# Scaling in two halves and a later add in a block's two even attentions, and another order with output by halves of tokens in its state space model

## The chip, the cores and the metric

The kernel runs on one core of one Trainium2 chip. The metric is the device time of one execution in microseconds (us). A core has five engines with a queue each: TensorE (PE; matmuls and transposes), VectorE (DVE), ScalarE (ACT), GpSimd (POOL) and SyncE (SP, which issues most DMAs). They run side by side and are held in order by semaphores alone: every instruction may count one up, and an engine waits until one has reached a value. All matmul results land in PSUM, which is four tiles of 1024 columns here (P0 to P3).

## What is computed

Two blocks in sequence, on 1024 tokens of width 1024, in float32. The first is a hybrid mixer (a state space model and a pooling branch), a cross attention and a feed-forward part; the second has an even layer with two kinds of attention of 8 heads each and an odd layer with windowed attention. The change touches the state space model and the attentions of the even layer:

```python
def ssd_chunked(xs, dt, a, bm, cm):          # chunks of 128 tokens, 16 heads of 64
    cb = jnp.einsum("bclgn,bcsgn->bgcls", cc, bc)
    y_diag = jnp.einsum("bghcls,bcsghp->bclghp", cb[:, :, None] * seg, xc)
    states = jnp.einsum("bcsgn,bghcs,bcsghp->bcghpn", bc, decay_states, xc)
...
    y_off = jnp.einsum("bclgn,cbghpn,bghcl->bclghp", cc, prev, jnp.exp(a_cs))
    return (y_diag + y_off).reshape(bsz, s, SSD_HEADS, p)
```

and, with y its result: y + d_skip * xs, times silu(z), an rmsnorm with the gain ssd_norm, and the product with w_out.

```python
def block(qi):                               # the even layer's attentions, per head
    sc = jnp.einsum('bqkgd,bskd->bkgqs', qi, k).astype(jnp.float32) * scale
    p = jax.nn.softmax(sc, axis=-1).astype(v.dtype)
    return jnp.einsum('bkgqs,bskd->bqkgd', p, v)
```

## The kernel before

Each float32 operand of a large product is split in a high part (float32r, copied by ACT: `XH`, `wh`, `PTH`) and a low part (the rest, made by DVE: `XL`, `wl`, `PTL`), and a product is three matmuls: high by high, high by low, low by high. The order of the work of every engine is written out by hand, one method per stage and engine (`pe_ssd`, `dve_ssd` and so on); the engines meet only through named counts, as ("bk", c) on DVE's.

**State space model** (`pe_ssd` L1116, `act_ssd` L1182, `pool_ssd` L1213, `dve_ssd` L1248). A loop over c = -1 to 7, in which n = c + 1 is the chunk prepared and c the chunk computed. PE, in a round: transposes of chunk n of XS into P0 (L280, "tx") and of B into P1; the mask products of n (L1143, "cb"); the product of the incoming state (L1150, "off", into P2); the 32 matmuls inside chunk c (L1104, "in", into P3); the new state of c (L1168, "st", into P2, over "off"); last the transposes of chunk c - 1's result back into P0 (`pe_back` L1108, "back"). P0 serves both transposes, so PE's "tx" of a round waits for the last reader of "back", which is DVE's addition `back(c)` at L1264 ("bk": back transposes plus the skip term, into XS). DVE, in a round: the scaled input of n (L1277), the masks (L1282), the scaled "off" (L1292), two products of the decay with the masks (L1258, "wgh"), y = P3 + off (L1299), the state's addition (L1304, "st"), and `back(c - 1)`. POOL: the decayed state (L1232), the decayed input (L1238), the skip product (L1242), and the gating of XS by silu(z) (L1226, "zx") three chunks behind; the gating of chunk 7 is DVE's (L1267). ACT: the decays, 16 + 2 instructions a chunk (L1206, L1211). SP: in the rounds 0, 1 and 4 it loads the rows of later chunks, in round 3 it reloads H, each behind PE's "in".

**Its output** (`pe_ssd_out` L1316, `act_ssd_out` L1322, `dve_ssd_out` L1349). When all of XS is gated, ACT makes eight high parts XH[:, j, :] of 1024 tokens (L1327), DVE the eight low parts (L1346), then both make the squares for the norm. PE's `pe_linear` (L342) goes through eight slabs of weights; the first two take 48 matmuls of 512 columns each, 6 for each k, and wait for the low part k. Behind the second come the roots of the norm (L453). XL shares its memory with the gates GZ. `pe_pair_by_halves` (L373), used so far by two other stages, does the first two slabs together, first for tokens 0 to 511 and then for 512 to 1023, waiting for the low part (name, k, 0) and (name, k).

**Even attentions** (`pe_attention` L2378, `act_attention` L2498, `dve_attention` L2574, `pool_attention` L2662). 128 blocks of 128 queries (64 for each kind of attention), software-pipelined over rounds n = 0 to 133. PE in round n: `turned(n - 3)`, the transposes of the scaled probabilities (L280: 8 of 128 columns into P2, in two groups d = 0, 1 of four, counted as ("t", n, d)); `scores(n)` (L2409, four matmuls in the first kind, six in the second); a side job in some rounds (`beside`: preparation of the second kind); half of a `values` product for a pair of blocks (L2422, L2423). ACT: the high parts PTH (L2548) of n - 3, the exponential of n - 1 (L2555, which also sums), a side job, and in the even rounds from 6 on the copy of one half of the values' result (L2569). DVE:

```python
for n in range(134):
    at = n - 2     # reciprocal L2641, behind ACT's ("exp", at)
    at = n - 3     # low parts PTL L1517, d = 0, 1
                   # reduction of the scores of n, L2648
                   # side job; weights
    if n % 2 == 0 and 0 <= n - 5 < 128:
        p = (n - 5) // 2
        e.wait_ge(*s.act.to(("half", p)))
        e.tensor_tensor(self.result(p), self.pv(p % 2)[0:64, 0:256], self.half(p % 2), ...)
```

The last statement is the add at L2659 ("o", p); PE's next use of that half of P3 waits for it. POOL scales the 1024 probabilities of a row block in place by the reciprocal, one instruction a block (L2669, ("sc", n)), behind the reciprocal; `turned(n)` waits for it.

Of the kernel before, what the change touches and what calls it, by code (L numbers as in the profile page):

```python
# [126 lines left out]
class Kernel:  # L127
# [988 lines left out]
    def pe_ssd(self, e):  # L1116
        sb, s = self.sb, self.s
        pt, pb, pm, py = self.P
        BC, XS = sb["BC"], sb["XS"]
        e.wait_ge(*s.act.to(("xs", 7)))  # L1120
        self.pe_place(e, 0)
        for c in range(-1, 8):
            n = c + 1
            cs, ns, u = slice(128 * c, 128 * c + 128), slice(128 * n, 128 * n + 128), c % 2
            if n < 8:
                if c > 1:
                    e.wait_ge(*s.dve.to(("bk", c - 2)))
                elif n:
                    e.wait_ge(*s.dve.to(("xc", n - 1)))
                for j in range(8):  # L1130
                    ins = self.turn(e, pt[:, 128 * j:128 * j + 128], XS[:, j, ns])
                ins.then_inc(*s.mm.up(("tx", n)))
                if n:
                    e.wait_ge(*s.act.to(("bt", n - 1)))
                    e.wait_ge(*s.dve.to(("wgh", n - 1, 1)))
                else:
                    self.pe_place(e, 1)
                if n < 7:
                    for g in range(2):
                        ins = self.turn(e, pb[:, 128 * g:128 * g + 128], BC[:, g, ns])  # L1140
                    ins.then_inc(*s.mm.up(("tb", n)))
                for g in range(2):
                    ins = e.matmul(pb[:, 512 + 128 * g:640 + 128 * g], BC[:, g, ns], BC[:, 2 + g, ns], start=True,  # L1143
                                   stop=True)
                ins.then_inc(*s.mm.up(("cb", n)))
            if c > 0:
                e.wait_ge(*s.dve.to(("st", c - 1)))
                for g in range(2):
                    gs = slice(512 * g, 512 * g + 512)
                    ins = e.matmul(pm[:, gs], BC[:, 2 + g, cs], sb["ST"][:, gs], start=True, stop=True)  # L1150
                ins.then_inc(*s.mm.up(("off", c)))
            if c >= 0:
                if c:
                    e.wait_ge(*(s.dve if c > 1 else s.act).to(("y", c - 1)))
                else:
                    self.pe_place(e, 3)
                self.pe_inside(e, c, 0)
                self.pe_inside(e, c, 1)
            if 0 <= c < 7:
                e.wait_ge(*s.act.to(("bt", c)))  # L1160
                e.wait_ge(*s.pool.to(("xd", c)))
                if c:
                    e.wait_ge(*s.dve.to(("yt", c)))
                else:
                    self.pe_place(e, 2)
                for g in range(2):
                    gs = slice(512 * g, 512 * g + 512)
                    ins = e.matmul(pm[:, gs], sb["BT"][u][:, 128 * g:128 * g + 128], sb["XD"][u][:, gs], start=True,  # L1168
                                   stop=True)
                ins.then_inc(*s.mm.up(("st", c)))  # L1170
            if c > 0:
                if n < 8:
                    e.wait_ge(*s.dve.to(("xc", n)))
                else:
                    e.wait_ge(*s.dve.to(("bk", c - 2)))
                self.pe_back(e, c - 1)
        e.wait_ge(*s.dve.to(("bk", 6)))
        self.pe_back(e, 7)
        self.emptied = {0: [(s.dve, ("bk", 7))], 1: [(s.act, ("bt", 6)), (s.dve, ("wgh", 7, 1))], 2: [(s.dve, ("yt", 7))],
                        3: [(s.dve, ("y", 7))]}  # L1180
# [67 lines left out]
    def dve_ssd(self, e):  # L1248
# [9 lines left out]
            e.tensor_tensor(x, x, cb, ALU.mult).then_inc(*s.dve.up(("wgh", n, g)))  # L1258

        def back(c):  # L1260
            x = XS[:, :, 128 * c:128 * c + 128]
            e.wait_ge(*s.mm.to(("back", c)))
            e.wait_ge(*s.pool.to(("skip", c)))
            e.tensor_tensor(x, pt.rearrange("p (j l) -> p j l", j=8), x, ALU.add).then_inc(*s.dve.up(("bk", c)))  # L1264
            if c == 7:
                e.wait_ge(*s.dve.here())
                e.tensor_tensor(x, x, self.sb["GZ"][:, :, 896:1024], ALU.mult).then_inc(*s.dve.up(("zx", 7)))  # L1267

        e.wait_ge(*s.act.to("tokens"))
        for c in range(-1, 8):  # L1270
# [25 lines left out]
            if c > 0:  # L1296
                e.wait_ge(*s.mm.to(("in", c, 1)))
                e.wait_ge(*s.dve.to(("yt", c)))
                e.tensor_tensor(YT, py, YT, ALU.add).then_inc(*s.dve.up(("y", c)))  # L1299
            if 0 <= c < 7:  # L1300
                e.wait_ge(*s.mm.to(("st", c)))
                if c:
                    e.wait_ge(*s.pool.to(("stm", c)))
                    e.tensor_tensor(ST, pm, sb["STM"][:, :], ALU.add).then_inc(*s.dve.up(("st", c)))  # L1304
                else:
                    e.tensor_copy(ST, pm).then_inc(*s.dve.up(("st", c)))
            if c > 0:
                back(c - 1)
        back(7)


# [4 lines left out]
    def pe_ssd_out(self, e):  # L1316
        between = {1: lambda e: self.pe_roots(e, "n1", self.T[2], self.s.dve.to(("n1", "sum", 7))),
                   2: lambda e: self.pe_spread(e, "n1", self.T[2])}
        self.pe_linear(e, "so", self.XH, self.XL, lambda k: [(self.s.lo, ("o", k))],
                       lambda j: [(self.s.dve, ("so", j))], between=between)  # L1320

    def act_ssd_out(self, e):  # L1322
        XS = self.sb["XS"]
        e.wait_ge(*self.s.pool.to(("zx", 6)))
        e.wait_ge(*self.s.dve.to(("zx", 7)))
        for j in range(8):
            e.activation(self.XH[:, j, :], XS[:, j, :], ACT.Copy,  # L1327
                         scale=self.vec("ssd_norm", j)).then_inc(*self.s.hi.up(("o", j)))
        for j in range(8):
            self.act_square(e, "n1", j, XS[:, j, :])  # L1330

        def empty(e, j):
            for i in {0: (), 1: (), 2: (0, 1, 2)}.get(j, (j,)):
                e.wait_ge(*self.s.dve.to(("h1", i)))
                e.dma_start(self.dr["hT"][:, i, :], self.H[:, i, :]).then_inc(*self.s.m[i // 4].up("out" if i % 4 == 3 else None))
                self.act_square(e, "n2", i, self.H[:, i, :])
                e.activation(self.AH[:, i, :], self.H[:, i, :], ACT.Copy,
                             scale=self.vec("xattn_norm", i)).then_inc(*self.s.hi.up(("x2", i)))

        between = {1: lambda e: self.act_roots(e, "n1", self.P[3][:, 0:8], 0, D, self.s.mm.to(("n1", "roots"))),  # L1340
                   2: lambda e: self.act_spread(e, "n1", self.T[3])}
        self.act_tiles(e, "so", empty, between)

    def dve_scaled_low(self, e, name, lo, src, gain, hi):
        e.wait_ge(*self.s.hi.to(name))
        e.scalar_tensor_tensor(out=lo, in0=src, scalar=gain, in1=hi.bitcast(F32), op0=ALU.mult,  # L1346
                               op1=ALU.subtract).then_inc(*self.s.lo.up(name))

    def dve_ssd_out(self, e):  # L1349
        XS = self.sb["XS"]  # L1350
        for j in range(8):
            self.dve_scaled_low(e, ("o", j), self.XL[:, j, :], XS[:, j, :], self.vec("ssd_norm", j), self.XH[:, j, :])
        for j in range(8):
            self.dve_square(e, "n1", j)

# [1022 lines left out]
    def pe_attention(self, e):  # L2378
        s = self.s
# [6 lines left out]
        def turned(n):  # L2386
            for d in range(2):
                if n:
                    e.wait_ge(*s.lo.to(("pt", n - 1, d)))
                elif d == 0:  # L2390
                    self.pe_place(e, 2)
                e.wait_ge(*s.pool.to(("sc", n)))
                for k in range(4):
                    c = 512 * d + 128 * k
                    ins = self.turn(e, self.P[2][:, c:c + 128], self.px(n)[:, c:c + 128])
# [178 lines left out]
    def dve_attention(self, e):  # L2574
# [59 lines left out]
        for n in range(134):  # L2634
            at = n - 2
            if 0 <= at < 128:
                w = sb["WST"][at % 4]
                e.wait_ge(*s.act.to(("exp", at)))
                if at > 3:
                    e.wait_ge(*s.pool.to(("sc", at - 4)))  # L2640
                e.reciprocal(w[:, 2:3], w[:, 1:2]).then_inc(*s.dve.up(("inv", at)))  # L2641
            at = n - 3
            if 0 <= at < 128:
                for d in range(2):
# [8 lines left out]
            for i, position in self.WEIGHTS.items():  # L2653
                if position == n:
                    self.dve_weights(e, self.no[i])
            if n % 2 == 0 and 0 <= n - 5 < 128:
                p = (n - 5) // 2
                e.wait_ge(*s.act.to(("half", p)))
                e.tensor_tensor(self.result(p), self.pv(p % 2)[0:64, 0:256], self.half(p % 2),  # L2659
                                ALU.add).then_inc(*s.dve.up(("o", p)))  # L2660

    def pool_attention(self, e):  # L2662

        s = self.s
        for n in range(128):
            r = self.sb["WST"][n % 4][:, 2:3].to_broadcast([128, 1024])
            e.wait_ge(*s.act.to(("exp", n)))
            e.wait_ge(*s.dve.to(("inv", n)))
            e.tensor_tensor(self.px(n), self.px(n), r, ALU.mult).then_inc(*s.pool.up(("sc", n)))  # L2669

    def dve_gate(self, e, j):
        O = self.sb["O"][:, j, :]
# [878 lines left out]
```

## Time and profile before

| what | us |
|---|---|
| median of 3 runs (lowest to highest) | 3027.79 (3027.22 to 3028.67) |
| profiled execution | 3027.36 |
| its span | 3025.5 |
| PE busy | 2891.0, 96% |
| DVE busy | 1731.7, 57% |
| ACT busy | 1243.9, 41% |
| POOL busy | 423.2, 14% |

Times in the profile are counted from the span's start. The state space loop takes about 467 to 562, the even attentions 1927 to 2408. "Busy" of an engine says how much of the span it ran an instruction; the time of the kernel goes by the chain of waits. A row's "[0.88 <-POOL T L2669]" says that the engine sat idle for 0.88 us just before, until POOL's instruction of line 2669 released it. Granted clock 1.00 is 2.4 GHz for PE, 0.50 is 1.2 GHz.

### The profile page before, as it was taken

How to read it: one execution, taken by the hardware profiler on the slowest of the kernel's cores; microseconds unless marked ns; L12 is line 12 of the kernel's file. 1: busy time of each engine (PE TensorE's matmuls, PEld its weight loads, DVE VectorE, ACT ScalarE, POOL GpSimd, SP SyncE). 2: the span in 40 equal slices, each digit the busy share in tenths (PEclk: the TensorE clock that was granted, in tenths of full speed). 3: DMA queues.
4: the chain of work that ended last, by engine and by line, in shares of the span. 5: the costliest groups of instructions: out<-in, count | busy, mean ns of one | idle time of the engine just before them, and what ended most of it. 6: DMA issues, size and time to landing. Idle time of an engine off the chain costs nothing.

```text
span 3025.5 us, 37063 instructions
## 1 busy us (share of the span) xinstructions
PE 2891.0 (96%) x14578; PEld 2413.6 (80%) x14578; DVE 1731.7 (57%) x2258; ACT 1243.9 (41%) x2028; POOL 423.2 (14%) x352
## 2 busy tenths in 40 slices
PE   8999998899999999999999999998999899999998
PEld 6877886687888888888888777787888787888976
DVE  6564476663554444444444745688888835317874
ACT  5221456332443111111112335577767724427851
POOL 0000005200000000000000000255544300004520
PEclk9999999999999999999999999999999999999999
DMA  4111334032222233322331222100001212131031
GB/s 145 56 42 50 126 105 184 26 118 84 91 63 72 73 91 98 92 81 75 87 93 42 76 88 63 56 1 5 15 15 39 98 59 88 49 91 57 22 112 70
DMA packets 226587, 219.28 MB, mean 72 GB/s; under 512 B 9456, under 2 KB 195056, under 8 KB 224880
## 3 DMA queue, kind: packets, MB, share of 16 engines
q1 hardware_dynamic: 214752, 174.90, 18.5%
q0 software_dynamic: 6912, 25.17, 2.8%
q10 hardware_dynamic: 4752, 16.84, 1.5%
q8 instruction: 118, 1.93, 0.3%
q14 instruction: 53, 0.43, 0.0%
HBM read 180.12 MB, written 34.67 MB: 71 GB/s over the span
## 4 chain that ended last, share of the span: by engine, by line
PE 86%; DVE 7%; ACT 3%; issue 2%; POOL 2%; DMA 0%; SPq 0%; ACTq 0%; DVEq 0%; POOLq 0%
PE P L342 61%; PE P L280 5%; PE P L2409 3%; PE P L311 2%; POOL T L2669 2%; PE P L283 1%; PE P L285 1%; PE P L284 1%; PE P L2423 1%; PE P L1104 1%; PE P L2422 1%; DVE PTL L1517 1%; DVE WST L2648 1%; PE P L3010 1%; PE P L1552 1%
## 5 line engine op out<-in xcount | busy, mean ns | idle before, releaser
L267 DVE TENSOR_TENSOR wl<-wf,wh 128x1024 fp32r<-128x1024 f32 (+4 forms) x239 | 251.6, 1053 | 923.8 <-ACT wh L259 923.5
L259 ACT ACTIVATE wh<-wf 128x1024 fp32r<-128x1024 f32 (+4 forms) x239 | 219.8, 920 | 1030.1 <-PE P L342 985.6
L342 PE MATMUL P<-AQ,wh 128*128 128x512 f32 x1824 | 489.4, 390 | 5.8 <-issue 3.0
L342 PE MATMUL P<-XH,wh 128*128 128x512 f32 (+1 forms) x1264 | 396.1, 395 | 8.9 <-DVE XL L1346 5.2
L342 PEld LDWEIGHTS P<-AQ,wh 128*128 128x128 f32 x1824 | 341.3, 188 | 77.9 <-issue 4.6
L342 PE MATMUL P<-XL,wh 128*128 128x512 f32 (+1 forms) x1264 | 391.2, 391 | 0.0
L342 PE MATMUL P<-XH,wl 128*128 128x512 f32 (+1 forms) x1264 | 391.2, 391 | 0.0
L2669 POOL TENSOR_TENSOR T<-T,WST 128x1024 f32<-128x1024 f32 x128 | 242.6, 1895 | 573.8 <-DVE WST L2641 573.8
L342 PEld LDWEIGHTS P<-XH,wh 128*128 128x128 f32 (+1 forms) x1264 | 235.7, 187 | 65.5 <-issue 14.6
L342 PE MATMUL P<-AQ,wl 128*128 128x512 f32 x912 | 280.8, 389 | 0.0
L342 PEld LDWEIGHTS P<-XL,wh 128*128 128x128 f32 (+1 forms) x1264 | 236.2, 187 | 52.6
L342 PEld LDWEIGHTS P<-XH,wl 128*128 128x128 f32 (+1 forms) x1264 | 236.1, 187 | 52.4
L342 PEld LDWEIGHTS P<-AQ,wl 128*128 128x128 f32 x912 | 171.2, 188 | 35.8
L1517 DVE TENSOR_TENSOR PTL<-P,PTH 128x512 fp32r<-128x512 f32 x256 | 164.7, 684 | 53.8 <-ACT PTH L2548 52.7
L342 PE MATMUL P<-FF,wh 128*128 128x512 f32 x680 | 182.4, 390 | 2.1 <-issue 2.0
L2548 ACT ACTIVATE PTH<-P 128x512 fp32r<-128x512 f32 x256 | 139.4, 595 | 84.4 <-PE P L280 81.8
L280 PE MATMUL P<-consts,T 128*128 128x128 f32 x1112 | 147.9, 277 | 26.4 <-POOL T L2669 23.5
L1698 POOL DMA_DIRECT2D AW<-ada_w x48 | 25.6, 534 | 996.4 <-DVE AA L1710 522.1
L2648 DVE TENSOR_REDUCE WST<-P 128x1 f32<-128x1024 f32 x128 | 155.7, 1217 | 2.2 <-PE P L2409 1.9
L280 PEld LDWEIGHTS P<-consts,T 128*128 128x128 f32 x1112 | 125.6, 142 | 38.5 <-DVE PTL L1517 22.2
L342 PEld LDWEIGHTS P<-FF,wh 128*128 128x128 f32 x680 | 127.3, 188 | 29.5 <-issue 2.9
L2555 ACT ACTIVATE T<-P,WST 128x1024 f32<-128x1024 f32 x128 | 143.4, 1120 | 0.1
(438 smaller groups left out, 5006.2 us busy)
## 6 DMA issues: line engine op xcount, KB each, us to landing
AW<-ada_w POOLq DMA_DIRECT2D x48, 512.0 KB, 4.1
wf<-w_gate_up SPq DMA_DIRECT2D x44, 512.0 KB, 3.8
H<-scratch_h SPq DMA_DIRECT2D x32, 512.0 KB, 6.5
wf<-w_in SPq DMA_DIRECT2D x28, 512.0 KB, 3.8
scratch_h<-H SPq DMA_DIRECT2D x24, 512.0 KB, 5.7
scratch_g<-T ACTq DMA_DIRECT2D x22, 512.0 KB, 3.0
wf<-odd_w_in SPq DMA_DIRECT2D x20, 512.0 KB, 3.8
wf<-even_w_in SPq DMA_DIRECT2D x17, 512.0 KB, 3.8
```

The lines of the kernel that those rows point to most:

```text
L259: e.activation(self.sb["wh"][i % 2][:, 0:m], self.sb["wf"][i % 2][:, 0:m], ACT.Copy).then_inc(*self.s.w_hi.up(i))
L267: e.tensor_tensor(l, f, h.bitcast(F32), ALU.subtract).then_inc(*self.s.w_lo.up(i))
L280: return e.transpose(out, in_, self.sb["consts"][p0:p0 + n, a + p0:a + p0 + n])
L283: e.matmul(out, wh, xh, start=first, stop=False)
L311: ins = e.matmul(self.P[slots[j]][:, t:t + 512], w, x[:, k, t:t + 512], start=first and k == 0, stop=last and k == kb - 1)
L342: ins = e.matmul(self.P[slot][0:m, t:t1], w, x[:, k, t:t1], start=first and k == 0, stop=last and k == kb - 1)
L1517: e.tensor_tensor(lo, src, hi.bitcast(F32), ALU.subtract).then_inc(*self.s.lo.up(name))
L2409: ins = e.matmul(p[:, ks], a[:, qs], c[:, ks], start=m == 0, stop=m == len(passes) - 1)
L2548: e.activation(self.probs("PTH", at, d), self.turned(d), ACT.Copy).then_inc(*s.hi.up(("pt", at, d)))
L2555: e.activation(self.px(at), self.P[at % 2], ACT.Exp, bias=w[:, 0:1], accum_out=w[:, 1:2]).then_inc(*s.act.up(("exp", at)))
L2648: e.tensor_reduce(sb["WST"][n % 4][:, 0:1], self.P[n % 2], AX, ALU.max, negate=True).then_inc(*s.dve.up(("max", n)))
L2669: e.tensor_tensor(self.px(n), self.px(n), r, ALU.mult).then_inc(*s.pool.up(("sc", n)))
```

## The change

In the state space loop PE does the transposes back of chunk c - 1 ahead of the new state of c, and DVE the addition `back(c - 1)` ahead of the state's addition. The output is made by halves of tokens: ACT makes eight high halves for tokens 0 to 511 as soon as PE has done "in" of chunk 7 and POOL has gated chunk 3, and eight more when everything is gated; DVE makes the low halves, the first four in between its last steps of the loop; PE takes the first two slabs of weights by halves. In the even attentions POOL scales in two instructions of 512 elements, each with its own count, PE's group d of transposes waits for half d, and the add of pair p moves on DVE from the end of round 2p + 6 to round 2p + 7, behind the reciprocal and ahead of the low parts. The number of instructions grows by 8 on ACT, 8 on DVE and 128 on POOL.

```diff
@@ pe_ssd
                 self.pe_inside(e, c, 0)
                 self.pe_inside(e, c, 1)
+            if c > 0:
+                if n < 8:
+                    e.wait_ge(*s.dve.to(("xc", n)))
+                else:
+                    e.wait_ge(*s.dve.to(("bk", c - 2)))
+                self.pe_back(e, c - 1)
             if 0 <= c < 7:
...
                 ins.then_inc(*s.mm.up(("st", c)))
-            if c > 0:
-                if n < 8:
-                    e.wait_ge(*s.dve.to(("xc", n)))
-                else:
-                    e.wait_ge(*s.dve.to(("bk", c - 2)))
-                self.pe_back(e, c - 1)
@@ dve_ssd, back(c)
             if c == 7:
-                e.wait_ge(*s.dve.here())
+                self.dve_out_low(e, 0, 2)
+                self.dve_out_low(e, 0, 3)
+                e.wait_ge(*s.dve.to(("bk", 7)))
                 e.tensor_tensor(x, x, self.sb["GZ"][:, :, 896:1024], ALU.mult).then_inc(*s.dve.up(("zx", 7)))
@@ dve_ssd
                 e.tensor_tensor(YT, py, YT, ALU.add).then_inc(*s.dve.up(("y", c)))
+            if c == 7:
+                self.dve_out_low(e, 0, 0)
+            if c > 0:
+                back(c - 1)
             if 0 <= c < 7:
...
-            if c > 0:
-                back(c - 1)
+        self.dve_out_low(e, 0, 1)
         back(7)
@@ pe_ssd_out
-        self.pe_linear(e, "so", self.XH, self.XL, lambda k: [(self.s.lo, ("o", k))],
-                       lambda j: [(self.s.dve, ("so", j))], between=between)
+        emptied = lambda j: [(self.s.dve, ("so", j))]
+        self.pe_pair_by_halves(e, "so", "o", emptied, {}, between)
+        self.pe_linear(e, "so", self.XH, self.XL, None, emptied, between=between, start=2)
@@ act_ssd_out
-        e.wait_ge(*self.s.pool.to(("zx", 6)))
-        e.wait_ge(*self.s.dve.to(("zx", 7)))
-        for j in range(8):
-            e.activation(self.XH[:, j, :], XS[:, j, :], ACT.Copy,
-                         scale=self.vec("ssd_norm", j)).then_inc(*self.s.hi.up(("o", j)))
+        e.wait_ge(*self.s.mm.to(("in", 7, 1)))
+        e.wait_ge(*self.s.pool.to(("zx", 3)))
+        for h in range(2):
+            ts = self.half_of(h)
+            if h:
+                e.wait_ge(*self.s.pool.to(("zx", 6)))
+                e.wait_ge(*self.s.dve.to(("zx", 7)))
+            for j in range(8):
+                e.activation(self.XH[:, j, ts], XS[:, j, ts], ACT.Copy,
+                             scale=self.vec("ssd_norm", j)).then_inc(*self.s.hi.up(("o", j) if h else ("o", j, 0)))
@@ dve_out_low (new) and dve_ssd_out
+    def dve_out_low(self, e, h, j):
+        ts = self.half_of(h)
+        self.dve_scaled_low(e, ("o", j) if h else ("o", j, 0), self.XL[:, j, ts], self.sb["XS"][:, j, ts],
+                            self.vec("ssd_norm", j), self.XH[:, j, ts])
...
+        for j in range(4, 8):
+            self.dve_out_low(e, 0, j)
         for j in range(8):
-            self.dve_scaled_low(e, ("o", j), self.XL[:, j, :], XS[:, j, :], self.vec("ssd_norm", j), self.XH[:, j, :])
+            self.dve_out_low(e, 1, j)
@@ pe_attention, turned(n)
-                e.wait_ge(*s.pool.to(("sc", n)))
+                e.wait_ge(*s.pool.to(("sc", n, d)))
@@ dve_attention
                 if at > 3:
-                    e.wait_ge(*s.pool.to(("sc", at - 4)))
+                    e.wait_ge(*s.pool.to(("sc", at - 4, 1)))
                 e.reciprocal(w[:, 2:3], w[:, 1:2]).then_inc(*s.dve.up(("inv", at)))
+            if n % 2 and n >= 7:
+                p = (n - 7) // 2
+                e.wait_ge(*s.act.to(("half", p)))
+                e.tensor_tensor(self.result(p), self.pv(p % 2)[0:64, 0:256], self.half(p % 2),
+                                ALU.add).then_inc(*s.dve.up(("o", p)))
             at = n - 3
...
-            if n % 2 == 0 and 0 <= n - 5 < 128:
-                p = (n - 5) // 2
-                e.wait_ge(*s.act.to(("half", p)))
-                e.tensor_tensor(self.result(p), self.pv(p % 2)[0:64, 0:256], self.half(p % 2),
-                                ALU.add).then_inc(*s.dve.up(("o", p)))
@@ pool_attention
-            r = self.sb["WST"][n % 4][:, 2:3].to_broadcast([128, 1024])
+            r = self.sb["WST"][n % 4][:, 2:3].to_broadcast([128, 512])
             e.wait_ge(*s.act.to(("exp", n)))
             e.wait_ge(*s.dve.to(("inv", n)))
-            e.tensor_tensor(self.px(n), self.px(n), r, ALU.mult).then_inc(*s.pool.up(("sc", n)))
+            for d in range(2):
+                x = self.px(n)[:, 512 * d:512 * d + 512]
+                e.tensor_tensor(x, x, r, ALU.mult).then_inc(*s.pool.up(("sc", n, d)))
```

## Rows read from the trace of the kernel before

**Rows 1.** The page's section 4: the chain that ended last, by engine.
```profile
PE 86%; DVE 7%; ACT 3%; issue 2%; POOL 2%; DMA 0%; SPq 0%; ACTq 0%; DVEq 0%; POOLq 0%
```

**Rows 2.** The chain in time, a state space round: start us, us, what.
```profile
506.68 1.31 PE P L280 x10
507.99 0.45 PE P L1143 x4
508.43 1.72 PE P L1150 x4
510.15 3.52 PE P L1104 x32
513.67 1.77 PE P L1168 x4
515.44 0.89 PE P L280 x8
...
516.62 1.22 DVE XS L1264
...
517.89 1.31 PE P L280 x10
```

**Rows 3.** The same chain, from the last state to the output projection.
```profile
548.90 1.24 DVE ST L1304
...
552.17 3.53 PE P L1104 x32
...
558.13 1.11 PE P L280 x8
...
564.45 24.86 PE P L342 x96
```

**Rows 4.** Two stretches: us, busy of each engine, granted clock, DMA share, GB/s.
```profile
505.00:515.00 10.00, 8.42 (x55) 6.64 (x55) 7.89 (x8) 6.94 (x19) 7.79 (x4) 1.00 0.07 9
565.00:575.00 10.00, 10.00 (x34) 7.98 (x33) 9.90 (x9) 9.17 (x10) 0.00 (x0) 0.72 0.00 0
```

**Rows 5.** PE's waits: for L2669 in all, and in 2076 to 2141 (us, times, longest).
```profile
  PE P L280: 23.5, 31
...
PE P L280 <- POOL T L2669: 6.6, 10, 0.9
```

**Rows 6.** PE's timeline: start, us, engine, line, operation, [idle before <-releaser].
```profile
2045.55 1.94 PE L280 MATMUL P<-consts,T 128*128 128x128 f32 x8 [2.95 <-POOL T L2669]
...
2095.87 1.06 PE L280 MATMUL P<-consts,T 128*128 128x128 f32 x8 [0.89 <-POOL T L2669]
2102.41 1.06 PE L280 MATMUL P<-consts,T 128*128 128x128 f32 x8 [0.88 <-POOL T L2669]
```

**Rows 7.** The timeline of a plain round of attention, DVE, ACT and POOL.
```profile
2098.37 1.21 DVE L2648 TENSOR_REDUCE WST<-P 128x1 f32<-128x1024 f32 x1
...
2098.83 0.38 ACT L2569 ACTIVATE TOK<-P 64x256 f32<-64x256 f32 x1
2099.27 1.09 ACT L2548 ACTIVATE PTH<-P 128x512 fp32r<-128x512 f32 x2
2099.62 0.42 DVE L2659 TENSOR_TENSOR O<-P,TOK 64x256 f32<-64x256 f32 x1
2100.07 0.16 DVE L2641 RECIPROCAL WST<-WST 128x1 f32<-128x1 f32 x1
2100.14 1.27 DVE L1517 TENSOR_TENSOR PTL<-P,PTH 128x512 fp32r<-128x512 f32 x2
...
2100.37 1.90 POOL L2669 TENSOR_TENSOR T<-T,WST 128x1024 f32<-128x1024 f32 x1 [2.26 <-DVE WST L2641]
```

**Rows 8.** Groups by form: count, busy us, mean ns, idle before: halves elsewhere.
```profile
L570 ACT ACTIVATE XH<-T,MOD 128x512 fp32r<-128x512 f32 x29 | 20.6, 723 | 30.5 <-DVE T L564 30.5
...
L576 DVE SCALAR_TENSOR_TENSOR XL<-T,MOD,XH 128x512 fp32r<-128x512 f32 x30 | 22.4, 748 | 1.3
```

**Rows 9.** The same view of POOL: the windowed attention's scaling, two sizes.
```profile
L3138 POOL TENSOR_TENSOR WS<-WS,WST 128x384 f32<-128x384 f32 x96 | 77.3, 829 | 49.1 <-DVE WST L3099 45.7 <-ACT HB L3072 3.3
...
L3138 POOL TENSOR_TENSOR WS<-WS,WST 128x256 f32<-128x256 f32 x32 | 19.0, 615 | 28.8 <-DVE WST L3099 28.8
```

## The prediction

> **What bounds the kernel now.** I read first the chain that ended last: 86% of it is TensorE (PE) [rows 1]. Time is won only where PE is made to wait, so I looked up the two places that the diff touches.
>
> In the state space stage the chain in order of time [rows 2] shows one round of PE: transposes of the next chunk 1.31 us, masks 0.45, state product 1.72, the 32 products inside the chunk 3.52, new state 1.77, transposes back 0.89. That is 9.66, but the round takes 11.21 (506.68 to 517.89): ahead of the next round's transposes PE waits 1.55 us for the addition at L1264 on VectorE (DVE). The same hole stands in the five rounds c = 1 to 5. At the end [rows 3] PE waits for the new state (548.90 to 550.18); the products of chunk 7 end at 555.70, and the output projection starts only at 564.45, 8.75 us later, after DVE and ScalarE (ACT) have done everything behind chunk 7. The granted clock of the 10 us from 565 on is 0.72 [rows 4]: 5.6 of them were at the lower level, 1.2 GHz, and before them PE had done next to nothing from 559.24 on.
>
> In the even attentions the waits [rows 5] say that PE waits for the scaling on GpSimd (POOL): 23.5 us in 31 waits over all rounds, 6.6 of it in the ten waits of 2076 to 2141, where the rounds are plain. In [rows 6] stand the wait of 0.88 us, which comes back every second round there (6.54 us for two rounds), and the longest of all, 2.95. The timeline [rows 7] shows where the lateness comes from: ACT copies the half at 2098.83, DVE's add runs at 2099.62 behind the reduction, the reciprocal only at 2100.07; POOL starts 0.30 after that and takes 1.90, and PE goes on 0.14 after its end, at 2102.41.
>
> **State space rounds.** I count from the end of the products inside a chunk. New order on PE: back transposes to 0.89, new state to 2.68. On DVE y runs from 0.04 to about 1.2, the addition L1264 (1.22) follows, since the back transposes arrive by then (the last set in rows 3 takes 1.11 with its handover), and ends at 2.4. PE is free at 2.68, so its wait of 1.55 is gone: the addition lies beside the state product. Late next is the state: its addition (1.24 in rows 3) now runs from 2.70 to 3.94, and PE wants it at 2.68 + 1.31 + 0.45 = 4.44, 0.5 us later. A round holds 7.89 x 1.121 = 8.8 us of DVE work, 8.7 of POOL's and 7.8 of ACT's [rows 4], all under 9.66, so they still fit; where the cover is short, part of the wait comes back. Five rounds give 5 x 1.55 = 7.8. From c = 6 to 7 no transposes cover the state, and it is made 0.89 later: **0.9 lost**. Net 6.9. The loads on SP's queue (rows of chunk 7, the reload of H) go with PE's signals, whose distance shrinks by 1.55 a round; their users are whole rounds behind. POOL's queue keeps its order.
>
> **Output by halves.** I count from the end T of chunk 7's products. PE turns chunk 6 back at once; DVE does y (to 1.2), the first low half, 0.75, for which ACT's first high half, 0.72 and started at once, is ready [rows 8], then the addition of chunk 6 (to 3.1); PE turns chunk 7 back from 3.1 to 4.2. There the projection starts: 4.2 instead of 8.75. It eats low halves as DVE makes them: the second is there at 3.8; the addition of chunk 7 is queued between, so the third comes at 6.2; the fourth at 6.8; the gating of chunk 7 to 8.0, then one each 0.67. PE lost 3.1 us to the clock in its 24.86 (half of the 5.6 in rows 4 and of the 0.55 ahead of them), so 96 matmuls are 21.8 us, three are 0.68. It waits 0.6 for the third low half and no more after it: half 0 ends at 15.7, and the first low half of the second set is there at 11.3. The end is at 4.2 + 21.8 + 0.6 = 26.6; now it is 8.75 + 24.86 = 33.6. **Gain 7.0.** The squares behind the low parts (seven additions of about 1.3 on DVE from 16.1, to 25.3) stay just ahead of the roots at 26.6; the eight more instructions on ACT and on DVE lie beside PE. The third slab's weights can be split from 25 on, when the first slab's tile is done, and PE wants them behind the roots at 28: covered by 0.7. Bounds: 3.9 if PE loses 3.1 to the clock again, 7.6 if nothing waits. I take 7.0, because the holes ahead are then 2.0 and 0.6 us, nearer to the rounds' 1.55, which keep the clock at 1.00 [rows 4], than to the 5.2 of now.
>
> **Attention.** The scaling of 1024 elements (1.90) becomes two of 512. No row has that size; POOL's other product with a broadcast takes 829 ns for 384 and 615 for 256 [rows 9], so 1.67 ns an element and 0.19 fixed: 1.04 for a half, 2.04 for both as they overlap a little. Bounds: 0.95 (half of 1.90) and 1.90 (no cheaper at all). I take 1.04, since 384 is near to 512. The Trainium skill's "GPSIMD Engine Reference", section 3.1, counts 2.6 cycles an element for two inputs and a dispatch for every instruction, which speaks against halving. By its figures a half is an estimated 1.11 us without the dispatch; the second half then comes some 0.2 us later than I say, and the plain rounds would keep a wait of about that.
>
> PE's first four transposes can start 0.86 us sooner after the reciprocal; the second four need both halves, 0.14 later than now, but only behind the first four (0.44). A wait that stays otherwise as it is thus shrinks by 0.3 at least and by 0.44 or so mostly. The add moves behind the reciprocal: without it in front, the reciprocal in rows 7 comes at 2099.50 instead of 2100.07, POOL starts at 2099.80, and its halves end at 2100.84 and 2101.84. PE was free at 2102.41 - 0.88 = 2101.53, wants the second half at 2101.97 and may have it at 2101.98. So in plain rounds the whole wait goes: a pair takes 5.66 us, while DVE's part of it is 5.17 (two of 0.08 + 1.21 + 1.13, and 0.33). The moved add waits for ACT's half, and the low parts are queued behind it: the half ends at 2098.83 + 0.38, the add would run from 2099.6 to 2100.0, and the low part starts at 2100.14 in any case. Cost nothing; 0.1 us a pair if that margin is gone. PE's side jobs use the bank that this add frees, and come 1.9 us into their round: covered.
>
> Sum: of the ten plain waits (6.6) I take 6.2. The other twenty short ones hold 23.5 - 6.6 - 2.95 = 14 us, in rounds with other work on DVE: at least 0.3 to 0.44 each (7), at most all; I take 9.8. The longest shrinks by 0.5, since DVE is late there for other reasons. **16.5 in all**, between 12 (the halves alone help) and 25 (all waits, and what PE loses to the lower clock behind the longest: its transposes take 1.94 there and 1.06 elsewhere [rows 6]).
>
> **Sum.** 6.9 + 7.0 + 16.5 = 30.4. The profiled execution took 3027.36 (its span 3025.5), so 2997.0 for one like it. The median of the three runs stands 0.43 above it: **2997.4 us**.
>
> **Rivals.**
> *The attention keeps its waits*: the second half, or the low parts behind the moved add, are late instead. Attention gives 3 to 6, the whole 18: 3009. For it: my margin for the second half is 0.01 us. Against: a late second half costs its lateness, not the whole wait.
> *The clock and the state eat into the first part*: PE loses its 3.1 us in the projection again, and the state's addition comes late in the rounds by 0.5: about 25 in all, 3003. The skill's "TensorE: Matmul & The Clock Gate", Part 1, says that an idle PE drops to half rate and gets the full one back only by sustained work. By that rule the hole of 2.0 us ahead of the last transposes may be enough, and the time is this rival's.
> *Slower, as a half costs POOL nearly what a whole does.* Then POOL needs 2 x 1.86 = 3.72 us a round where a plain round takes 3.27: over the 64 rounds of the first attention 29 lost, 14 gained in front, 3043. It decides from (3.27 + 14/64)/2 = 1.74 us for a half. Against: 829 ns for 384 elements.
> *Nothing to speak of*: what is won is given back behind it, as later stages wait for weights that come at a pace of their own. Against: rows 1 leaves little that is not PE.
>
> **How the numbers follow.** Forecast 0.75; waits stay in attention 0.10; clock and state 0.08; nothing 0.04; slower 0.03. A measurement of this kernel can tell about 0.2% (6 us) from no change. The forecast's own bounds are 2988 (all waits of attention gone) to 3004 (12 there, 11 in front); for 8 in 10 I reach on to the first rival: 2989 to 3010. Faster by over 0.2% (below 3021.7) takes the first three cases, 0.93; same 0.04; slower 0.03.
>
> **What would show it.** Right: L1264 every 9.66 us with no wait of PE for it; the projection's first matmul 4.2 us after the last product of chunk 7, at 2.4 GHz; 256 scalings of 1.04 us; plain pairs of 5.66; PE's waits for POOL under 7 us in sum. Wrong: PE waiting for the second half or the low parts in most rounds, a wait for the state's addition, halves above 1.2 us, or a gain that returns as a wait in the next stage.

## The result, and the profile after

The changed kernel takes 3001.96 us (median of 4, 2998.70 to 3004.56), the kernel before 3027.93 in the same series (4, 3027.22 to 3028.67): 26.0 us less, ratio 0.9916 with a 95% interval of 0.9904 to 0.9928. The profiled execution is its fastest: 2998.70, with a span of 2996.9, 28.6 below the span of before.

The page's section 4, the chain that ended last, by engine, against [rows 1]; and from its section 5 the scaling, with count, busy us, mean ns, idle before:

```profile
PE 89%; DVE 5%; ACT 2%; issue 2%; POOL 1%; DMA 0%; SPq 0%; ACTq 0%; DVEq 0%; POOLq 0%
...
L2691 POOL TENSOR_TENSOR T<-T,WST 128x512 f32<-128x512 f32 x256 | 261.2, 1042 | 541.3 <-DVE WST L2661 518.3
```

A half costs 1042 ns, as taken. One round of the state space loop in the chain in order of time (start us, us, what), against [rows 2]:

```profile
505.26 3.52 PE P L1104 x32
508.78 0.88 PE P L280 x8
509.66 1.72 PE P L1174 x4
511.38 1.16 PE P L280 x10
512.54 0.45 PE P L1143 x4
512.98 1.72 PE P L1150 x4
514.70 3.52 PE P L1104 x32
```

A round is 9.44 us and all of it is PE's: the addition, now L1265, is gone from the chain. The end of the loop in the same view, against [rows 3]:

```profile
537.08 0.88 PE P L280 x8
...
539.72 1.24 DVE ST L1311
...
542.98 3.53 PE P L1104 x32
...
549.61 1.10 PE P L280 x8
550.74 1.22 DVE XS L1265
...
573.81 1.68 PE P L453 x16
```

Chunk 7's products end at 546.51, the first two slabs at 573.81, 27.3 us later; before it was 33.6. In the timeline the projection's first matmul is at 550.46 (4.0 behind the products), then PE waits for the third low half:

```profile
549.63 2.84 POOL L1226 TENSOR_TENSOR XS<-XS,GZ 128x1024 f32<-128x1024 f32 x1 [7.73 <-DVE XS L1265]
...
550.46 0.48 PE L283 MATMUL P<-XH,wh 128*128 128x512 f32 x1
...
551.88 1.80 DVE L1359 SCALAR_TENSOR_TENSOR XL<-XS,vecs,XH 128x512 fp32r<-128x512 f32 x2
...
553.08 0.50 PE L283 MATMUL P<-XH,wh 128*128 128x512 f32 x1 [0.98 <-DVE XL L1359]
```

The clock stood at 1.00 there (the view by stretches; columns as in [rows 4], where it was 0.72):

```profile
550.00:560.00 10.00, 9.02 (x43) 7.20 (x42) 9.48 (x13) 6.64 (x12) 2.47 (x1) 1.00 0.01 2
```

PE's waits from 1890 to 2410, the even attentions (us, times, longest), against [rows 5]:

```profile
PE P L280 <- DVE PTL L1537: 6.5, 5, 2.9
...
PE P L280 <- POOL T L2691: 4.4, 12, 0.4
```

POOL's 23.5 us are 4.4, but the transposes' waits for the low parts rose from 1.1 to 6.5; the one wait of 3.2 us for the add at L2665 is as long as before. A pair of plain rounds (timeline) is 5.73 where it was 6.54, and the add now stands behind the reciprocal:

```profile
2075.20 1.27 PE L280 MATMUL P<-consts,T 128*128 128x128 f32 x8
...
2075.92 0.15 DVE L2661 RECIPROCAL WST<-WST 128x1 f32<-128x1 f32 x1
2076.10 0.42 DVE L2665 TENSOR_TENSOR O<-P,TOK 64x256 f32<-64x256 f32 x1
2076.22 2.04 POOL L2691 TENSOR_TENSOR T<-T,WST 128x512 f32<-128x512 f32 x2 [0.51 <-DVE WST L2661]
...
2080.93 1.07 PE L280 MATMUL P<-consts,T 128*128 128x128 f32 x8
```

### The profile page after: what moved, and what is told of

It is laid out like the page before. It is cut to its first block, busy times and chain, and to the rows that moved or that the text cites. A ratio compares the mean times of both kernels' runs of the same rounds, so it can differ in the third digit from the quotient of the medians.

```text
span 2996.9 us, 37208 instructions
## 1 busy us (share of the span) xinstructions
PE 2885.4 (96%) x14578; PEld 2408.4 (80%) x14578; DVE 1730.6 (58%) x2266; ACT 1248.2 (42%) x2036; POOL 442.1 (15%) x480
## 4 chain that ended last, share of the span: by engine, by line
PE 89%; DVE 5%; ACT 2%; issue 2%; POOL 1%; DMA 0%; SPq 0%; ACTq 0%; DVEq 0%; POOLq 0%
PE P L342 61%; PE P L280 5%; PE P L2429 4%; PE P L311 2%; PE P L283 2%; PE P L285 2%; PE P L284 2%; PE P L2443 2%; PE P L2442 1%; PE P L1104 1%; PE P L3032 1%; PE P L1572 1%; ACT wh L259 1%; PE P L2158 1%; PE P L3026 1%
## 5 line engine op out<-in xcount | busy, mean ns | idle before, releaser
L342 PE MATMUL P<-XH,wh 128*128 128x512 f32 (+1 forms) x1232 | 384.7, 394 | 3.7 <-DVE TMP L1381 2.5
L342 PE MATMUL P<-XL,wh 128*128 128x512 f32 (+1 forms) x1232 | 380.5, 390 | 0.0
L342 PE MATMUL P<-XH,wl 128*128 128x512 f32 (+1 forms) x1232 | 380.2, 390 | 0.0
L2691 POOL TENSOR_TENSOR T<-T,WST 128x512 f32<-128x512 f32 x256 | 261.2, 1042 | 541.3 <-DVE WST L2661 518.3
L342 PEld LDWEIGHTS P<-XH,wh 128*128 128x128 f32 (+1 forms) x1232 | 228.8, 186 | 58.6 <-issue 9.2
L342 PEld LDWEIGHTS P<-XH,wl 128*128 128x128 f32 (+1 forms) x1232 | 229.5, 186 | 51.0
L342 PEld LDWEIGHTS P<-XL,wh 128*128 128x128 f32 (+1 forms) x1232 | 229.4, 186 | 51.0
```

The costliest lines, as they stand in the source:

```text
L342: ins = e.matmul(self.P[slot][0:m, t:t1], w, x[:, k, t:t1], start=first and k == 0, stop=last and k == kb - 1)
L2691: e.tensor_tensor(x, x, r, ALU.mult).then_inc(*s.pool.up(("sc", n, d)))
```

## The experiments

For every kernel I took PE's matmuls in their order (14578 in each trace; the eight more of "transposes twice" are left out) and subtracted the start of the k-th from its start in the kernel before. What this lead grows by in a stretch is what the kernel gained there; stretches by the times of before:

```
lead gained, us      to 472  472-590  590-1100  1100-1200  1200-1929  1929-2411  2411-2900
                            (state space)     (feed-forward)         (attentions)
changed kernel          1.2     14.3      -0.1       -1.6        1.1       13.3        0.2
order alone             0.6      9.2      -1.6       -1.6       -1.1       -0.1       -0.7
order and output        0.9     14.2       0.0       -1.6       -1.2       -0.1       -0.7
output alone            0.5      6.4      -1.7       -1.6        0.0        0.5        0.0
attentions alone       -1.4      0.3       0.0        0.0        0.1       15.7       -1.8
halves alone            0.8      0.1       0.0        0.0        0.0        9.1       -2.0
add alone              -1.6      0.3       0.0        0.0        0.1        5.9       -2.1
state first            -1.1     14.7      -0.1       -1.6       -1.3       14.4       -1.7
low part later         -1.0     14.4      -0.1       -1.6        1.0       17.6       -0.1
both                   -0.3     14.9       0.0       -1.6       -1.1       18.0       -1.7
transposes twice       -1.9     13.9      -0.1        0.0       -0.1       13.3        0.3
changed, once more      0.9     14.2       0.0       -1.6       -1.2       14.4       -1.7
```

The first column is the same code in all and says how far two executions differ for no reason of the kernel's: from 1.9 us slower to 1.2 faster. Each row is one execution, the one that was profiled.

Of the attentions the same holds, on a larger scale. Five of these traces have the same attention code (changed kernel twice, attentions alone, state first, transposes twice) and gain 13.3 to 15.7 us. They differ in how long PE ran at the lower clock in the rounds, summed from the granted clock without the stretch at their end, which every trace has: 13.7 us where 13.3 are gained (both times), 10.2 us where 14.4 are (both times), 6.8 us where 15.7 are; the kernel before has 13.7. So about 13.3 is what the edit itself brought at an equal clock, and what is over it goes with the clock. The same wait of the same code, in the changed kernel's two traces, cost the clock in the first (granted 0.57 from 1958 to 1962) and not in the second (1.00 from 1960 to 1964):

```profile
1957.41 1.54 PE L280 MATMUL P<-consts,T 128*128 128x128 f32 x8 [1.69 <-DVE PTL L1537]
```

```profile
1960.35 1.25 PE L280 MATMUL P<-consts,T 128*128 128x128 f32 x8 [1.69 <-DVE PTL L1537]
```

**The turned order alone**: the hunks of `pe_ssd` and the move of `back(c - 1)` in `dve_ssd`.

> The state space loop's turned order alone (PE and DVE), output and attentions as before. Theory (the parts add up, each worth what its stretch of the trace after the change shows): five rounds of 9.45 us in place of 11.21 (8.8 us), 1.2 lost at the last state, so 7.6 us faster than before, with the output projection still starting 8.75 us after the products of chunk 7 and at the lower clock. Rival (the clock gives it back, or later stages wait): the loop is as much shorter in the trace but the whole gains under 4 us.

Measured: 3023.21 against 3026.84, ratio 0.9988 [0.9979, 0.9997], 3.6 us. The trace has the gain where it should be, and the rival has what became of it. 8.0 us are gained by the end of chunk 7's products; the projection still starts 8.7 us behind them, but its 96 matmuls take 23.68 us in place of 24.86, because less of them ran at the lower clock: 9.2 in all. Then 1.6 go where the clock falls behind an idle time of 2.54 us at 596.53, and 3.5 in later stages that the change does not touch.

**Order and output**: all hunks of the state space model, none of the attentions.

> Turned order and output by halves, attentions as before. Theory: 14.3 us faster than before (8.0 to the end of chunk 7's products, 6.3 in the first two slabs), that is 6 to 7 more than the order alone; first matmul of the projection 4 us after chunk 7's products at 2.4 GHz. Rival: the output by halves adds under 3 us, since the squares and the roots end last.

Measured: 3015.92, ratio 0.9964 [0.9952, 0.9977], 10.9 us. The stage gains 14.2 as in the changed kernel, 3.6 of it are lost behind it. The output by halves is worth 7.3 us more than the order alone in the medians. The theory's 14.3 for the whole was not reached.

**Attentions alone**: the hunks of `turned`, `dve_attention` and `pool_attention`.

> Both edits of the even attentions, state space model as before. Theory: 13.3 us faster than before (what the stretch from the first scores to the even output lost in the trace after the change); PE's waits for POOL near 4 us in place of 23.5, and 7 us of waits for the low parts. Rival (attention and state space model are not independent, the clock's low stretches shift): under 10 or over 16 us.

Measured: 3014.53, ratio 0.9957 [0.9944, 0.9969], 12.3 us. PE's waits are 4.4 us for POOL and 6.9 for the low parts. The stretch gains 15.7, and the next loses 1.8. With the 10.9 of the state space part the sum is 23.2 against 26.0: within their intervals the two add up.

**Halves alone**: as before, with the add where it was.

> POOL scales in two halves, the add stays at the end of the even rounds. Theory (the add ahead of the reciprocal is half of the lateness): a plain pair of rounds shortens from 6.54 by 0.3 to 0.44 us, and the waits that stay come each pair; 8 us faster than before. Rival (the halves are all of it): as fast as both edits, within 2 us. Second rival (PE only waits for the second half instead): under 4 us.

Measured: 3020.07, ratio 0.9975 [0.9966, 0.9984], 6.8 us; 9.1 in the stretch. Its plain pairs (PE's timeline) are 6.08 us, 0.46 shorter where 0.3 to 0.44 were foretold, with the second half awaited once in each, so the first theory holds:

```profile
2088.60 0.63 PE L280 MATMUL P<-consts,T 128*128 128x128 f32 x4 [0.37 <-POOL T L2671]
...
2094.68 0.63 PE L280 MATMUL P<-consts,T 128*128 128x128 f32 x4 [0.37 <-POOL T L2671]
```

**The add alone**: POOL's instruction whole, the add in the odd rounds.

> The add a round later alone; POOL scales 1024 elements in one instruction as before, state space model as before. Both edits of the attentions gave 12.3 us of the median, the halves alone 6.8. Theory (two parts of one chain that add up): some 5 us faster than before, PE's waits for POOL at 14 to 17 us, a plain pair of rounds between 5.9 and 6.1 us since the reciprocal comes 0.57 sooner, and no new wait for the low parts. Rival (the add was ahead of the reciprocal only in rounds whose lateness another work sets): under 2 us.

Measured: 3023.21 against 3027.04, ratio 0.9987 [0.9978, 0.9996], 3.8 us; 5.9 in the stretch. A plain pair is 5.97 us, PE's waits for POOL in the attentions are 18.3, more than the 14 to 17 foretold, and none for low parts appears in plain rounds. 9.1 + 5.9 = 15.0, where both give 13.3 to 15.7: the parts add up, within what the clock adds.

```profile
2084.78 1.07 PE L280 MATMUL P<-consts,T 128*128 128x128 f32 x8 [0.17 <-POOL T L2669]
...
2090.75 1.06 PE L280 MATMUL P<-consts,T 128*128 128x128 f32 x8 [0.17 <-POOL T L2669]
```

**Output by halves alone**: the loop's order as before.

> Output by halves alone, the loop's order and the attentions as before. Theory: the first two slabs gain 6.3 us as in the changed kernel (projection's first matmul 4 us after the last product of chunk 7, hole ahead of the last transposes 2.2 us), whole 5 to 7 us faster than before. Rival (it needs the turned order, because the loop leaves DVE or POOL late for chunk 7): gain under 3 us, the gating of chunk 6 or the squares end last. The clock after the hole of 2.2 us tells the third: if it falls to 1.2 GHz here, the full clock in the changed kernel was luck, and 3 us of the gain are gone.

Measured: 3026.88 against 3027.04, ratio 0.9998 [0.9989, 1.0007]: no gain that can be told. The trace of one execution has the 6.4 us in the stretch and loses 3.3 of them behind it. That execution, 3023.24, is the fastest of its eleven; the other ten took 3025.92 to 3027.63, and what they lost more was not seen. So the theory holds for the stage and fell for the whole. The clock behind the idle time of 2.23 us stayed up here. In the medians the output alone gives 0.2 us and the order alone 3.6, but both together 10.9: here the parts do not add up, though their stages do nearly (6.4 + 9.2 for 14.2). Both traces lose 1.6 to 1.7 us between 590 and 1100, behind the same idle time of 2.54 us, where the trace with both edits loses nothing.

**State first in round 6**: in `pe_ssd` and `dve_ssd` of the changed kernel the guard of the moved steps, with the old place for this one round:

```diff
-            if c > 0:
+            if c > 0 and c != 6:
                 back(c - 1)
...
+            if c == 6:
+                back(c - 1)
```

> The changed kernel, but in the round c = 6, which has no next transposes, PE and DVE take the new state first and the transposes back after it, as before the change. Theory: the products of chunk 7 end 0.9 to 1.2 us earlier after those of chunk 6 than in the changed kernel (9.4 us there), with no new wait behind them. Rival: the transposes back, now beside the state's addition, push the product with the state by as much, and nothing is won.

Measured, one execution: 3004.24, beside 3027.04 for before. The gain is there, at 0.83 us (0.9 to 1.2 foretold): chunk 7's products end 8.6 us behind chunk 6's again. But only 0.4 of it are left at 590 (14.7 against 14.3), since the clock was at its lower level when the last transposes came:

```profile
551.10 1.97 PE L280 MATMUL P<-consts,T 128*128 128x128 f32 x8 [2.23 <-DVE XS L1268]
```

**The queries' low part later**: DVE's `dve_low` of RQL in `beside` moves behind the reduction of the next round, and the weights of the even output go from round 92 to 98.

```diff
-    WEIGHTS = {("rv", 1): 57, ("qk", 1): 88, ("eo", 0): 92, ("eo", 1): 121}
+    WEIGHTS = {("rv", 1): 57, ("qk", 1): 88, ("eo", 0): 98, ("eo", 1): 121}
...
-                self.dve_low(e, job, sb["RQL"][:, :], x, sb["RQH"][:, :])
...
+        def rest(n):
+            job = n > 0 and self.beside(n - 1)
+            if job and job[0] == "rope end":
+                self.dve_low(e, job, sb["RQL"][:, :], self.T[3], sb["RQH"][:, :])
...
+            rest(n)
```

> The changed kernel, with the low part of the rotated queries (1.23 us of DVE, behind a wait of 1.1 for ACT's high part) a round later, in rounds 34 and 93 instead of 33 and 92, and the weights of the even output split in round 98 instead of 92. In the changed kernel PE still waits 2.95 us in round 34 for low parts, and 3.2 us in round 93 for the add. Theory (DVE is late in these two rounds because of this work, not because of the scaling or the add): both waits go or shrink under 1.5 us, 3 to 6 us faster than the changed kernel, 29 to 32 faster than before. Rival (the wait moves to the next round): the sum of PE's waits in the attentions shrinks by under 2 us.

Measured: 2999.48, ratio 0.9907 [0.9894, 0.9921], 27.6 below before, where 29 to 32 were foretold. PE's two long waits shrink, the 2.95 for low parts to 1.6 and the 3.2 for the add to 1.2, but a new one of 1.2 for the add appears; the three sums below are 11.8 in place of 14.1, so 2.3 us less, just over the rival's 2:

```profile
PE P L280 <- DVE PTL L1537: 5.1, 6, 1.7
PE P L280 <- POOL T L2696: 4.3, 11, 0.8
PE P L283 <- DVE O L2669: 2.4, 2, 1.2
```

The attentions' gain in the trace, 17.6 us, is 3 to 4 more than the changed kernel's; but this trace had only 6.8 us at the lower clock there. Beside "attentions alone", which had as much and gains 15.7, it is 1.9 more.

**Both of these**:

> The changed kernel with both of the improvements tried: state first in round c = 6, and the queries' low part a round later with the output's weights split in round 98. Theory (parts of two stages add up): 0.8 us before the products of chunk 7 and 4.3 us in the attentions over the changed kernel, so 3 to 5 us faster than the changed kernel on the same chip. Rival (PE's clock gives part of it back, as it did with the turned order alone): under 2 us.

**The changed kernel once more, on the same chip**:

> The changed kernel once more, on the chip of the two above: 24 to 28 us faster than before. In its trace the hole of 2.2 us ahead of the last transposes of the state space model may cost the clock or not; if it does, the projection's first slabs gain some 1.5 to 3 us less than the 6.3 of the first trace.

Measured: both together 2999.78 (4 runs, 2995.94 to 3000.97), ratio 0.9908 [0.9894, 0.9921]; the changed kernel 3001.52 (5 runs, 2998.07 to 3002.41), ratio 0.9913 [0.9900, 0.9927], before 3027.45. The stages gain 32.9 us against 28.6 (14.9 + 18.0, 14.2 + 14.4), but of the 4.3 more only 1.7 arrive in the medians, and the runs overlap: the rival's number. The trace with both edits had only 3.4 us at the lower clock in the attentions' rounds, the changed kernel's second trace 10.2, and PE's three kinds of waits are 12.7 us (6.5, 3.8 and 2.4) for 14.1 in the changed kernel's first and 14.6 in its second: so part of the 4.3 is the clock of one execution, not the edit. Both versions with the later low part have lower medians than the changed kernel; that either is faster is not settled.

**Transposes twice**: PE turns chunk 7 back once more ahead of `pe_back(e, 7)`.

```diff
         e.wait_ge(*s.dve.to(("bk", 6)))
+        e.wait_ge(*s.dve.to(("y", 7)))
+        for j in range(8):
+            self.turn(e, self.P[0][:, 128 * j:128 * j + 128], self.T[3][:, 128 * j:128 * j + 128])
         self.pe_back(e, 7)
```

> The changed kernel, in which PE does the transposes back of chunk 7 twice (0.9 us of PE on the path). It asks why 1.6 us are lost in the feed-forward part by every kernel with a changed state space part: PE idles 1.98 us there in all kernels, and only in those the clock falls behind it. Theory (it is a matter of when the hole comes, not of what was changed): with the shift of 0.9 the clock may stay at 2.4 GHz behind that hole, and 1.6 us come back: the whole is 0.7 faster to 0.9 slower than the changed kernel. Rival (the clock falls there whatever the shift): 0.9 slower and the loss of 1.6 stays in the trace.

Measured: 3003.50 (5 runs), 2.0 above the changed kernel on the same chip, where 0.9 above was the theory's end; why the medians lie so far apart was not seen. But the loss at 1100 to 1200 is gone from its trace. The same four matmuls behind the same idle time (the profile shows nothing that ended it), in PE's timelines of the kernel before, of the changed kernel, and of this one:

```profile
1140.59 1.17 PE L342 MATMUL P<-FF,wh 128*128 128x512 f32 x4 [1.98 <-issue]
```

```profile
1125.15 1.85 PE L342 MATMUL P<-FF,wh 128*128 128x512 f32 x4 [1.98 <-issue]
```

```profile
1128.72 1.16 PE L342 MATMUL P<-FF,wh 128*128 128x512 f32 x4 [1.98 <-issue]
```

So the clock's fall there does not follow from the changed code itself; that it goes by when the idle time comes fits this one trace, and is not shown further. The extra transposes were cheap. All sixteen took 1.97 us, at a granted clock of 1.00, and PE then waited 0.58 us for the third low half in place of 0.98:

```profile
552.71 1.97 PE L280 MATMUL P<-consts,T 128*128 128x128 f32 x16 [2.23 <-DVE XS L1268]
```

The stage gains 13.9 where the same code without them gains 14.2 and 14.3.

## Why the prediction was right

Foretold were 30.4 us and 2997.4, measured 26.0 and 3001.96, in the range of 2989 to 3010; the mechanisms of the forecast are the ones that the traces show, but two of its three terms were too large, and one too small. By its steps:

- **Rounds.** 5 x 1.55 was taken, 5 x 1.77 came (11.21 to 9.44): the ten transposes that no longer follow a wait take 1.16, not 1.31. The cover held, with no wait of PE for the state in the rounds. The loss at the last state is 0.83 (9.43 for 8.60), as taken (0.9). From the products of chunk 0 to those of chunk 7 the gain is 8.0; 6.9 was the term.
- **Output.** Taken 7.0, measured 6.3 (33.6 to 27.3). The start is 4.0 us behind the products (4.2). The clock stayed up, as I chose, but that was not certain: of the eight traces with this idle time of 2.23 us, six kept it and two lost it. The mis-sized step is the third low half: I had 0.75 us for it and 0.6 for PE's wait; beside POOL's gating the DVE instruction took up to 1.14, and PE waited 0.98, which cost 1.3 us between the starts of its matmuls. The squares ended ahead of the roots, as foretold.
- **Attention.** Taken 16.5, measured 13.3 in the profiled execution; of the 13.3 to 15.7 in the five with this code, what is over 13.3 goes with less time at the lower clock. The cost of a half (1042 ns) and the plain pairs (5.66 taken, 5.73 measured) were right, and POOL's waits are under the 7 us named. Too large was what I took for the other waits. The longest did not shrink by 0.5: it is 2.95 again, because DVE's low parts are late there, not the scaling. Of the twenty short ones I took 9.8; there the low parts came in as the next thing late (6.5 us of waits for them in place of 1.1). The margin of 0.01 us for the second half held in the plain rounds.
- **Sum.** The three terms come to 27.6 us (8.0 + 6.3 + 13.3) in place of 30.4, so most of what was missed is the attentions' 3.2. The rest is a step that I had not written down: that a stage's gain stays. The two stages gain 27.6 us and 28.6 (14.2 + 14.4) in the two traces of this code, and 26.0 and 25.9 arrive in the medians. 1.6 are lost in the feed-forward part in both traces, where the clock falls. The other stages that the change does not touch add up to a gain of about 2.5 in the first trace, the fastest execution of its series, and to a loss of 2.0 in the second, with 1.2 of it between 1200 and 1929 and 1.7 behind the attentions. The rival "nothing to speak of" had the right kind of thing (given back later) and the wrong cause; the clock rival had the clock, but in the wrong place.

By the figures of the Trainium skill's "GPSIMD Engine Reference", section 3.1, a half was an estimated 1.11 us and a dispatch; the trace has 1.04, and the wait of 0.2 us a plain round did not come. With the Trainium skill's "TensorE: Matmul & The Clock Gate", Part 1, the traces agree in that PE's clock falls behind idle time; but the idle time of 2.23 us ahead of the last transposes cost it in two traces (state first, both) and not in the six others that have it, the changed kernel's two among them.

What stays open: what the other executions of "output alone" lost, and by what the clock's fall behind a given idle time could be foretold.

## What to carry to other kernels

Ask of each engine's order whether the instruction that another engine waits for stands behind one that nobody waits for yet: two moves of that kind gave 8.0 and 5.9 us in the traces of their stages. Splitting a producer pays when its fixed cost is small (0.19 of 1.04 us) and the consumer starts on the first part; then find out what is late next, here the low parts. And price a gain of a few us as uncertain by what PE's clock gives back in other stages, some 1.6 us at a time. A stage's gain has to be read in the stage, with how long the clock was low there beside it (2.4 us between traces of one and the same attention code went with that), and the whole over many runs.

## What the runs showed of the hardware

- The same idle time of 1.98 us in the feed-forward part left PE's clock at 2.4 GHz in the kernel before and in the three with edits of the attentions alone, and cost 1.6 us in all seven kernels with a changed state space part, the changed kernel twice; in the eighth, shifted by its extra transposes, it did not.
- Other idle times of PE were also followed by the lower clock in some traces and not in others: 1.69 us in the attentions in one of the changed kernel's two, 2.23 us ahead of the last transposes in two of eight, and 2.53 to 2.54 us behind the first slabs of the output in two of all thirteen (order alone, output alone).
- POOL's gating of XS takes 2.35 to 2.39 us in the kernel before; its last one in the changed kernel takes 2.84, while DVE makes a low half from two operands in SBUF, which takes up to 1143 ns in place of 741. In three kernels where the third low half starts behind the gating (state first, both, transposes twice) it takes 0.74 us; the gating takes 2.82 to 2.83 there too, beside the second low half, which takes 0.74. The Trainium skill's "GPSIMD Engine Reference", section 8, says that GpSimd shares its SBUF interfaces with VectorE and names just such instructions; the trace agrees.
